# A TensorE depthwise convolution and a later norm scale in a fused four-layer fp32 model kernel

## The reference, cut to what matters

```python
u = h @ w_pw1 + b_pw1
a, gate = jnp.split(u, 2, axis=-1)
u = a * jax.nn.sigmoid(gate)
u = jnp.pad(u, ((0, 0), (CONV_WIDTH - 1, 0), (0, 0)))        # CONV_WIDTH = 31
u = lax.conv_general_dilated(u, w_dw[:, None, :], (1,), 'VALID', feature_group_count=D_MODEL, ...) + b_dw
u = jax.nn.silu(layer_norm(u, ln_g, ln_b))
return u @ w_pw2 + b_pw2
```

## Time and profile before

| | us |
|---|---|
| median of 3 runs | 1336.02 (1332.59 to 1343.74) |
| span of the profiled execution | 1335.0 |
| PE, DVE, ACT, POOL busy | 1241.4, 929.1, 699.9, 311.4 |
| `pw1` starts, `pw2` starts | 17.85, 144.15 |
| last up product of the first gated layer ends, down starts | 932.1, 935.88 |

### The profile page before, as it was taken

The page is one execution under the profiler, slowest core; times in us unless marked ns, Lnnn a source line. Parts: engine busy times, 40 slices in busy tenths (PEclk is TensorE's granted clock), DMA queues, the critical chain, the costliest instruction groups (busy, mean ns, idle before and its releaser), DMA issues.

```text
span 1335.0 us, 25143 instructions
## 1 busy us (share of the span) xinstructions
PE 1241.4 (93%) x9780; PEld 1020.2 (76%) x9780; DVE 929.1 (70%) x1462; ACT 699.9 (52%) x1112; POOL 311.4 (23%) x303
## 2 busy tenths in 40 slices
PE   8695899999899999999999999998899999999896
PEld 6584778888675788888766668887788557887786
DVE  6799787765783886655893347777777545777775
ACT  5581566633555566533553455555564455655552
POOL 7983020000212100000202322444230033244400
PEclk9897999999998999999998899999999969999999
DMA  7420135455260545555341024443575312455352
GB/s 296 179 90 37 49 125 205 189 193 207 103 246 8 190 165 214 189 189 195 145 170 59 31 96 149 178 184 143 179 262 197 127 64 86 168 189 189 130 173 75
DMA packets 16342, 202.34 MB, mean 152 GB/s; under 512 B 1808, under 2 KB 3088, under 8 KB 3216
## 3 DMA queue, kind: packets, MB, share of 16 engines
q1 hardware_dynamic: 16272, 201.38, 40.6%
HBM read 200.33 MB, written 1.05 MB: 151 GB/s over the span
## 4 chain that ended last, share of the span: by engine, by line
PE 57%; issue 16%; DVE 13%; POOL 8%; ACT 4%; DMA 2%; POOLq 0%; SPq 0%; DVEq 0%; ACTq 0%
PE ps L528 13%; PE ps L529 13%; PE ps L530 13%; PE ps L682 5%; POOL tmp L1569 4%; DVE w_lo L1631 4%; DVE xn L1839 3%; POOL f_lo L1539 2%; PE ps L715 2%; ACT w_hi L1085 2%; POOL qT L1539 2%; PE ps L693 1%; DVE stat L1641 1%; DMA staged<-weights 1%; PE ps L539 1%
## 5 line engine op out<-in xcount | busy, mean ns | idle before, releaser
L1631 DVE SCALAR_TENSOR_TENSOR w_lo<-staged,w_hi 128x2048 f16<-128x2048 f32 (+2 forms) x189 | 425.4, 2265 | 63.2 <-ACT w_hi L1085 63.1
L528 PE MATMUL ps<-f_hi,w_hi 128*128 128x256 f16 x1628 | 445.0, 273 | 23.0 <-DVE tmp L2120 11.9
L1085 ACT ACTIVATE w_hi<-staged 128x2048 f16<-128x2048 f32 (+2 forms) x189 | 350.4, 1869 | 194.3 <-PE ps L530 172.7
L530 PE MATMUL ps<-f_hi,w_lo 128*128 128x256 f16 x1628 | 444.5, 273 | 0.0
L529 PE MATMUL ps<-f_lo,w_hi 128*128 128x256 f16 x1628 | 444.5, 273 | 0.0
L528 PE MATMUL ps<-x_hi,w_hi 128*128 128x256 f16 x1064 | 291.1, 274 | 11.2 <-ACT m L1235 10.6
L529 PE MATMUL ps<-x_lo,w_hi 128*128 128x256 f16 x1064 | 291.1, 274 | 0.0
L530 PE MATMUL ps<-x_hi,w_lo 128*128 128x256 f16 x1064 | 291.0, 273 | 0.0
L528 PEld LDWEIGHTS ps<-f_hi,w_hi 128*128 128x128 f16 x1628 | 159.4, 98 | 54.0 <-DVE tmp L2120 22.5
L529 PEld LDWEIGHTS ps<-f_lo,w_hi 128*128 128x128 f16 x1628 | 159.6, 98 | 19.1
L530 PEld LDWEIGHTS ps<-f_hi,w_lo 128*128 128x128 f16 x1628 | 159.6, 98 | 18.8
(11 more groups left out here) (236 smaller groups left out, 1616.6 us busy)
## 6 DMA issues: line engine op xcount, KB each, us to landing
staged<-weights SPq DMA_DIRECT2D x82, 2048.0 KB, 7.5
staged<-weights SPq DMA_DIRECT2D x16, 1408.0 KB, 6.0
staged<-weights SPq DMA_DIRECT2D x2, 1024.0 KB, 9.2
cst<-constants SPq DMA_DIRECT2D x1, 1029.0 KB, 16.6
h<-x_turned SPq DMA_DIRECT2D x1, 1024.0 KB, 4.8
out<-xn SPq DMA_DIRECT2D x8, 128.0 KB, 2.0
vec<-vectors SPq DMA_DIRECT2D x1, 811.0 KB, 6.2
cst<-constants SPq DMA_DIRECT2D x1, 129.5 KB, 4.7
```

The source lines that it names most:

```text
L528: pe.matmul(out, wh, xh[:, c, :], start=(c == 0), stop=False)
L530: last = pe.matmul(out, wl, xh[:, c, :], start=False, stop=(c == kc - 1))
L1085: act.activation(w_hi[:, s, o:o + n], staged[:, s, o:o + n], ACT.Copy, scale=SW).then_inc(hi_split, 1)
L1631: dve.scalar_tensor_tensor(w_lo[:, s, o:o + n], staged[:, s, o:o + n], SW, w_hi[:, s, o:o + n], ALU.mult, ALU.subtract).then_inc(lo_split, 1)
```

## The change

Convolution: all 31 taps go to PE as banded fp16 products. Taps are taken four at a time (8 steps). `copy_rows(j)` makes, with 16 fp32 matmuls of 32x32 (one for each of 4 groups of 32 channels and 4 shifts), four shifted copies of each channel group, stacked on the partitions. ACT and DVE split them into fp16 (`shift`). `convolve(j)` adds 8 steps x 3 products x 4 groups, each 128 rows by 32 columns, into the four 32-partition bands of one bank. The banded weights (hi and lo, 1024 columns for a chunk each) are made once in the head by DVE for chunks 0 to 2 and by POOL for chunks 3 to 7. `pw1`, copies and convolution alternate on PE, over three banks for `pw1`. The layer norm's sums are made over bands and tokens; mean and inverse root are worked out in 12 small columns `by_token` and spread by PE (`rows_of`). The vectors load in two parts, the big attention weights last. The split of the last `pw2` half moves behind the layer norm.

Gated layers: `scale_gates` goes; the second norm scale is put in at the down product (one more DVE instruction for each of its eight outputs). DVE takes the up product a pair later, from four banks; ACT's `hi` runs one half further ahead and between the up product and the silu; the down weights are split in halves of 1408 columns, and PE waits for each half by itself.

```diff
+TAP_SET = 4
+BAND = P // TAP_SET
+TAP_STEPS = -(-TAPS // TAP_SET)
+SHIFTED = T + TAP_SET * (TAP_STEPS - 1)
+PADDED = 288
...
+            def copy_rows(j):
+                pe.wait_ge(glu, j + 1)
+                for r in range(2):
+                    if j:
+                        pe.wait_ge(shift_lo, 2 * j - 1 + r)
+                    for tap in range(TAP_SET):
+                        for g in (2 * r, 2 * r + 1):
+                            at = slice(BAND * g, BAND * g + BAND)
+                            last = pe.matmul(ps[BAND * tap:BAND * tap + BAND, 4 + g, 0:SHIFTED], cst[at, BAND * g:BAND * g + BAND],
+                                             u_rows[at, j % 4, tap:tap + SHIFTED], start=True, stop=True)
+                    last.then_inc(copies, 1)
+            def convolve(j):
+                if j < VECTOR_BANDS:
+                    pe.wait_ge(dve_banded, 2 * (j + 1))
+                else:
+                    pe.wait_ge(pool_banded, 2 * (j + 1 - VECTOR_BANDS))
+                pe.wait_ge(shift_lo, 2 * j + 2)
+                if j:
+                    pe.wait_ge(conv_drained, 2 * j - 1)
+                for step in range(TAP_STEPS):
+                    for e, (w, x) in enumerate(((0, 0), (0, 1), (1, 0))):
+                        for g in range(TAP_SET):
+                            last = pe.matmul(ps[BAND * g:BAND * g + BAND, 3, 0:T], banded[w][:, (j * TAP_SET + g) * TAP_STEPS + step, :],
+                                             shifted[:, j % 2, x, g, TAP_SET * step:TAP_SET * step + T],
+                                             start=(step == 0 and e == 0), stop=(step == TAP_STEPS - 1 and e == 2))
+                last.then_inc(conv_product, 1)
...
-            linear("pw1", 4, x_hi, x_lo, done=2)
...
+            for j in range(1, DC):
+                gate_or_value(2 * j)
+                copy_rows(j - 1)
+                gate_or_value(2 * j + 1)
+                convolve(j - 1)
+            copy_rows(DC - 1)
+            sum_bands(range(0, 4))
+            sum_bands(range(4, 6))
+            convolve(DC - 1)
...
-                        wait_from(pe, u_drained[layer], i * 4 + (n - 1))
-                        features(ps[:, 2 + j, 0:T], sl, (2 * j + 1) * DC * P, DC, *g_in).then_inc(u_product[layer], 1)
+                        wait_from(pe, u_drained[layer], i * 4 + (n - 3))
+                        features(ps[:, 2 + n, 0:T], sl, (2 * j + 1) * DC * P, DC, *g_in).then_inc(u_product[layer], 1)
...
+                pe.sem_inc(down_taken[layer], 2)
...
+                    def fresh(c):
+                        if c == 0:
+                            pe.wait_ge(lo_split, i * 4 + (2 * (u0 + s) + 1))
+                        if c == GC // 2:
+                            pe.wait_ge(lo_split, i * 4 + (2 * (u0 + s) + 2))
+                        if s == 0 and (c % 8 == 0 or c == GC - 2):
+                            pe.wait_ge(p_lo_ready[layer], GC if c == GC - 2 else min(c + 8, GC - 2))
+                    return fresh
                 with pe.Fori(0, dict(STREAM)[down] // 2) as i:
...
+                        features(ps[:, s, 0:T], (u0 + s) % 2, 0, GC, f_hi, f_lo, gated(s, i)).then_inc(product[down], 1)
...
+                for r in range(2):
+                    act.wait_ge(copies, 2 * j + r + 1)
+                    if j >= 2:
+                        act.wait_ge(conv_product, j - 1)
+                    act.activation(shifted[:, j % 2, 0, 2 * r:2 * r + 2, :], ps[:, 4 + 2 * r:6 + 2 * r, 0:SHIFTED], ACT.Copy,
+                                   scale=SX).then_inc(shift_hi, 1)
...
+                        act.wait_ge(u_drained[layer], i * 4 + n)
+                        act.activation(f_hi[:, bass.ds(i * 4 + (n - 1), 1), :], tmp[:, 3 - j:4 - j, :], ACT.Copy,
+                                       scale=SF).then_inc(p_hi_ready[layer], 1)
+                    if new:
+                        act.wait_ge(u_product[layer], i * 4 + (n + 1))
+                        hi(g, g // 2 % 2, i * 16 + 16 * (g // 4 + 1), size, o + size * (g % 2))
...
-            for n in range(DIAGS):
-                pool.tensor_scalar(diagonal(n), k("ident"), v("taps", DC * (n % TAPS) + CONV_TENSOR[n // TAPS]), None,
-                                   ALU.mult).then_inc(pool_diag, 1)
...
+            pool.wait_ge(taps_split, 2)
+            n = TAP_STEPS * TAP_SET
+            for c in range(VECTOR_BANDS, DC):
+                for e in range(2):
+                    pool.tensor_tensor(banded[e][:, n * c:n * c + n, :], k("band").unsqueeze(1).to_broadcast([P, n, BAND]),
+                                       tap_parts[:, e, n * c:n * c + n].unsqueeze(2).to_broadcast([P, n, BAND]),
+                                       ALU.mult).then_inc(pool_banded, 1)
...
-            def scale_gates(layer):
-                pool.wait_ge(inverted, NORM_AT[f"ffn2_{layer}"] + 1)
-                with pool.Fori(0, GC // 2) as i:
-                    for j in range(2):
-                        pool.wait_ge(g_silu[layer], i * 2 + (j + 1))
-                        pool.tensor_tensor(tmp[:, j, :], tmp[:, j, :], LATE_SCALE, ALU.mult).then_inc(g_normed[layer], 1)
...
-            step(dve.memset(u_pad, 0.0))
+            step(dve.memset(u_rows, 0.0))
+            dve.wait_ge(taps_split, 1)
+            dve.scalar_tensor_tensor(tap_parts[:, 1, :], v("conv_taps", 0, TAP_STEPS * DC * TAP_SET), SW, tap_parts[:, 0, :],
+                                     ALU.mult, ALU.subtract).then_inc(taps_split, 1)
+            dve.wait_ge(taps_split, 2)
+            n = TAP_STEPS * TAP_SET
+            for c in range(VECTOR_BANDS):
+                for e in range(2):
+                    dve.tensor_tensor(banded[e][:, n * c:n * c + n, :], k("band").unsqueeze(1).to_broadcast([P, n, BAND]),
+                                      tap_parts[:, e, n * c:n * c + n].unsqueeze(2).to_broadcast([P, n, BAND]),
+                                      ALU.mult).then_inc(dve_banded, 1)
...
+                for r in range(2):
+                    dve.wait_ge(shift_hi, 2 * j + r + 1)
+                    dve.scalar_tensor_tensor(shifted[:, j % 2, 1, 2 * r:2 * r + 2, :], ps[:, 4 + 2 * r:6 + 2 * r, 0:SHIFTED], SX,
+                                             shifted[:, j % 2, 0, 2 * r:2 * r + 2, :], ALU.mult, ALU.subtract).then_inc(
+                        shift_lo, 1)
...
+                if j:
+                    shift(j - 1)
                 dve.wait_ge(drained["pw1"], 2 * j + 2)
-                dve.tensor_tensor(u_pad[:, j, TAPS - 1:TAPS - 1 + T], m[:, 2 * (j % 2), :], m[:, 2 * (j % 2) + 1, :],
+                if j >= 4:
+                    dve.wait_ge(copies, 2 * (j - 3))
+                dve.tensor_tensor(u_rows[:, j % 4, TAPS - 1:TAPS - 1 + T], m[:, 2 * (j % 2), :], m[:, 2 * (j % 2) + 1, :],
-            taps(TAPS * DC, DC)
...
+            dve.wait_ge(conv_product, DC)
+            c = DC - 1
+            dve.tensor_scalar(conv[:, c, :], ps[:, 3, 0:T], INV, v("b_dw", c), ALU.mult, ALU.add).then_inc(last_conv, 1)
...
+            dve.reciprocal(by_token[:, 8:10], by_token[:, 6:8]).then_inc(ln_step, 1)
+            centre(1)
+            centre(2)
+            dve.wait_ge(ln_rows, 2)
             for c in range(DC + 3):
                 if c < DC:
-                    dve.tensor_tensor(conv[:, c, :], conv[:, c, :], stat[:, 1, :], ALU.mult).then_inc(ln_scaled, 1)
+                    dve.wait_ge(ln_centred, c + 1)
+                    dve.tensor_tensor(conv[:, c, :], conv[:, c, :], ps[:, 7, 0:T], ALU.mult).then_inc(ln_scaled, 1)
+                if c + 3 < DC:
+                    centre(c + 3)
                 if c >= 3:
                     x_lows("layer_norm", c - 3, (x_hi, x_lo))
+            split(2 * u0 + DC + 3)
...
-                        dve.wait_ge(p_hi_ready[layer], i * 4 + n)
-                        at = bass.ds(i * 4 + (n - 1), 1)
-                        dve.scalar_tensor_tensor(f_lo[:, at, :], tmp[:, 3 - j:4 - j, :], SF, f_hi[:, at, :], ALU.mult,
-                                                 ALU.subtract).then_inc(p_lo_ready[layer], 1)
+                        dve.wait_ge(u_product[layer], i * 4 + n)
+                        dve.wait_ge(g_silu[layer], i * 4 + n)
+                        dve.scalar_tensor_tensor(tmp[:, 3 - j, :], ps[:, 2 + (n - 1) % 4, 0:T], INV, tmp[:, 1 - j, :],
+                                                 ALU.mult, ALU.mult).then_inc(u_drained[layer], 1)
+                        o, size = halves
+                        lo(g // 2 % 2, g % 2, i * 4 + (g + 1), size, o + size * (g % 2))
...
-                        g = 2 * u0 + n + 3
-                        lo(g // 2 % 2, g % 2, i * 4 + (g + 1))
-                    if new:
-                        dve.wait_ge(u_product[layer], i * 4 + (n + 1))
-                        dve.wait_ge(g_normed[layer], i * 4 + (n + 1))
-                        dve.scalar_tensor_tensor(tmp[:, 2 + j, :], ps[:, 2 + j, 0:T], 1.0, y, ALU.mult,
```

(11 more changed lines are left out.)

352 lines of the change are left out of this document (153 added, 199 removed).

## The result

The changed kernel takes 1290.72 us (median of 4 runs, 1276.51 to 1296.11), the kernel before 1334.3 (4 runs beside it). The ratio is 0.9636, 95% interval [0.9559, 0.9713]: 43.6 us faster, where 21 were forecast. Both kernels' times vary with the clock that TensorE is granted: four executions of the changed kernel spanned 1274.6 us at 0.979, 1286.7 at 0.968 and 1290.9 and 1294.2 at 0.962. Medians here are of all executions, while a ratio and its 95% interval leave out those in a slower state that every kernel falls into at times (a lower granted clock and a time over 1.5% above its fastest).

The account below looks back on a forecast made before the run. PE was taken to bound the kernel, busy 1241.4 of 1335.0 us. Taking off 18 for the gated layers and 3 for the convolution gave 1314, plus 1.0 for the span's distance from the median 1315 us; range 1293 to 1338.

Parts of the forecast that it names:

- Gated layers, the sum: Both gated layers: PE waits removed, 11.9 + 6 + 2.1 - 1.0 = 19 us gained, taken as 18.
- the wait ahead of the down part: Gated layers: PE's wait for the last gate drain, 7.5 us less some 1.5 for two starts, gains 6.
- the added down instruction: Gated layers: one more DVE instruction per down output; only the last counts, 0.5 us, twice.
- The bound of 20: Gated layers: upper end of the 13 to 20 us set around the forecast gain of 18.
- The load's slack: Gated layers: weight half lands at 10.9 us, ACT asks at 13.2, so hidden with 2.3 us to spare.
- The head: Convolution's start: DVE and POOL band products take turns, so the last x_lo ends at 47, 24 us later.
- The loop: Convolution: value product 5.24, copies and convolution 3.6, tile changes 0.6 make 9.5 us of PE a chunk.
- The tail: From the last value product's end at 121.4 to `pw2`: 19.0 us, so `pw2` starts at 140.4.
- (1): Cheap head, DVE keeping POOL out: convolution gains 20 to 25 us instead of 3, total 1295; chance 0.19.
- (2): POOL's products slower than fp32 ones, or a chunk needs 11 us instead of 9.5: 1325 to 1337; chance 0.16.
- (3): Column bands run one behind the other: a chunk takes 20 us, 75 us more, total 1390; chance 0.07.
- (4): Gated layers keep their wait, silu late behind ACT's earlier half or its load: 12 of 18 us stay, 1327; chance 0.08.

Follow-up runs that it names:

- own_gate: Changed kernel, with TensorE made to wait in each gated pair until VectorE has drained that pair's gate product before the up product; 1330.66 us, one run.
- pool_types: Changed kernel plus 18 extra POOL multiplications of six kinds into a free buffer in the last gated layer; 1301.74 us, one run.
- bands_in_row: Changed kernel with the convolution's loops turned, all 24 products of one column band before the next band; 1340.4 us, ratio 1.0139 to the kernel before.

## Why the prediction was wrong

Forecast 1315, measured 1290.7: 24 us too slow. The direction and both mechanisms were right; the sizes of both halves were not, the gated layers by 12 us and the convolution by 10 to 11.

**Gated layers, the sum: 19 (taken as 18), measured 30.0.** That PE bounds the pairs behind the change is right: no wait for DVE or POOL is left, and the layer runs at PE's own pace. The failed step is the price of the waits. I added idle rows as if they were the time that a stall takes. The earlier trace rows hold 21.5 us in 41 waits; own_gate shows that each costs 0.16 to 0.17 more than its row, 6.7 us for 41. That gives 28.2. I had also discounted the wait ahead of the down part from 7.5 to 6 and charged 1.0 for the added down instruction; neither showed. What is then left of the 30.0 is the second layer's clock, 0.99 before and 1.00 after: behind the 3.8 us wait ahead of its down part PE made 16 steps at 0.213 us, which cost 1.7 us (behind the same wait of the first layer it made none). The bound of 20 was no bound, since it was made of the same rows. The check was there: in the timeline of before the pairs' stalls end at 912.14, 917.85, 923.62 and 929.32 us, 5.7 apart, against the 5.24 that I had worked out. 38 stalls of 0.47 are 17.9 us, not 11.9. The last of the four:

```profile
929.32 0.28 PE L528 MATMUL ps<-f_hi,w_hi 128*128 128x256 f16 x1 [0.29 <-DVE tmp L2120]
```

The load's slack was also misadded: a load that goes out at 3.1 us and takes 7.5 lands at 10.6 and not at 10.9, which changed nothing.

The Trainium skill, "Perfetto Trace Analysis", section "Tensor Engine Instruction (MATMUL, LD_WEIGHTS)", says that the end of a matmul is estimated and not observed. No run here shows a matmul's true end. What the runs do show fits the page, a record of 0.273 us where the next matmul starts 0.109 later, and own_gate gives what follows from it for a stall.

**The head: 24 us lost, in fact 17.** The taking of turns is right, and right per instruction of any length: 2.84 against 1.14 us a step, and even a 64-column scaling waited 1.7 us. The hold of POOL's product was off, 2.4 instead of 1.7. I took it from plain 256-column additions, as four times 0.60, with 2.7 for the recorded time. pool_types has 2.42 recorded for plain operands and 1.97 for the banded kind, of which 1.7 is held; so some 0.3 of the 0.7 us was in the extrapolation and 0.4 in the broadcast operands. The 0.60 was itself too much: it left DVE 0.27 of a turn, while the sum charged DVE's own products in full. Taken as the 1.7 was, a turn less DVE's time alone, the rows of before give 0.87 - 0.40 = 0.47. Ten times 0.7 is 7.0, and all that followed came 6.8 us earlier, x_lo's, unit 2 and convolve(0). The Trainium skill's "GPSIMD Engine Reference", section "Elementwise — side-by-side cycle accounting", gives 2.6 cycles an element for two inputs, an estimated 2.2 us for 1024 at the 1.2 GHz that it names, without the start; the plain kinds agree (2.40 and 2.18), and it has no word on broadcast ones, so the runs decide.

**The loop: 9.5 us a chunk, in fact 8.88.** 5.24 + 2.74 + 0.69 + 0.21. The convolution's 2.7 is right, the copies were 0.2 and the changes of tile 0.4 too dear. Six periods forecast 58.8 us from the start of convolve(0) to that of convolve(6); it took 56.1, 112.3 - 56.2, although the first period was 11.7 (convolve(0) ran at the lower clock, 5.31 us). 2.7 us.

**The tail: 18.6, in fact 18.0** (112.3 to 130.3). The 19.0 of the forecast ran from the end of the last value product at 121.4, which is 0.4 ahead of the start of convolve(6), 121.8, from which the loop is counted here.

6.8 + 2.7 + 0.6 = 10.1, the distance between 140.4 and 130.3. The gain was 13.9 and not 3 since I had also charged 0.5 us for DVE being late to drain `pw2`'s first output and rounded down: from `pw2`'s start to the first mark it is 23.9 us in both kernels.

**The rivals.** (1) named 1295, near the result, and for a wrong reason: behind the first of its products, which was there before POOL's, DVE never got two in a row while POOL had one waiting. (2), a slower POOL or chunk, and (3), bands one behind the other, fell; bands_in_row shows what (3) would have been for the convolutions alone, 55 us and not 75, since in it the copies stay parallel. The Trainium skill's 2.38 times for three bands of 512 columns ("TensorE: Matmul & The Clock Gate", Part 3) is less than these runs show for four bands of 256: they do 96 matmuls in 2.74 us against the 10.5 of 96 steps, 3.8 times. (By the 2.38 a convolution would be an estimated 4.4 us; the prediction's 4.3 is a slip.) The same part has the rule that a weight load overlaps running matmuls only where the row groups differ. It is not borne out for bands that share all rows: at 0.0285 us a matmul the loads of the next band can't have stood still for a 0.109 us stream each time. (4) fell.

**The range**, 1293 to 1338, missed by 2 us. It took in rival (1), with 20 to 25 us from the convolution, but no case in which the gated layers give more than 20; the terms leaned the same way, a lower bound on the waits' price and upper bounds on the costs.

## What to carry to other kernels

Price a stall of TensorE by the repeat time of the loop (5.7 us against 48 steps of 0.109), not by its idle rows: each of those is short by the recorded length of a matmul less the step. When a producer is late by a fraction of a microsecond, either a shorter chain or one stage of slack takes the whole gain, so do the simpler one. Before two engines that take turns get one-time work at the start, count their turns on the path, put one of them behind the path, and look for a split that the next load waits for: here three small edits brought the first mark 20.7 us forward.

## What the runs showed that was not expected

- Three attention stages, the same instructions in all kernels, took 73.9 to 82.2 us (in the first model, granted clock 1.00 to 0.90), 131.0 to 142.1 (1.00 to 0.92) and 136.2 to 141.5 (0.93 to 0.89) between the same marks. Together that is more than most parts of the change; what sets it off in one execution and not in another stayed open and was not tried.
- A POOL product with both inputs broadcast is quicker than one with plain operands, 1.97 us for 1024 columns against 2.40 with fp32 and 2.18 with fp16 inputs.
- DVE and POOL alternate by whole instructions: a 0.19 us scaling of 64 columns took 1.88 beside a POOL product, a 2.2 us split 3.9. The reciprocal of 256 columns did not take part, 1.74 us beside a POOL product.
- When PE's queue goes from one column band to the next, the first matmuls of the new band run beside the last of the old one: 9.33 us for 96 in four rows of 24, where 96 steps of 0.109 make 10.5.
